# Two FFN blocks in one order: both high halves, then both low halves; a row of scales by turning a column

## The chip, the cores and the metric

One core of one Trainium2 chip. The metric is the device time of one launch in microseconds (us), the median of the runs. TensorE multiplies matrices, ScalarE applies functions and copies, VectorE does elementwise arithmetic, GpSimd and SyncE issue transfers; each works through its own program in order and waits on semaphores for the others.

## The reference

Two blocks of a model on 256 tokens of width 1024, in float32. Cut to the part that the change touches:

```python
def rms_norm(x, g):
    y = xf * lax.rsqrt(jnp.mean(xf * xf, axis=-1, keepdims=True) + RMS_EPS)
    return (y * g.astype(jnp.float32)).astype(x.dtype)

def swiglu(x, w_gate, w_up, w_down):
    return (jax.nn.silu(x @ w_gate) * (x @ w_up)) @ w_down

# first block, layers 0 and 1
h = h + 0.5 * swiglu(rms_norm(h, ffn1_norm[i]), ffn1_w_gate[i], ffn1_w_up[i], ffn1_w_down[i])
h = h + m          # layer 0: a gated recurrence, layer 1: pooling over windows
h = h + 0.5 * swiglu(rms_norm(h, ffn2_norm[i]), ...)
h = h + sigmoid(rms_norm(h, ple_norm[i]) @ ple_w_gate[i]) * (p[i] @ ple_w_proj[i])
# second block, layers 0 and 1: a mix of attention and a bidirectional recurrence, then
x = x + (jax.nn.silu(h @ w_gate[layer]) * (h @ w_up[layer])) @ w_down[layer]
```

The hidden width of every FFN is 2816. There are six FFNs: they are followed by the recurrent stage, a PLE stage (the gate with `p`), the pool, a PLE stage, a mix stage and the end of the program.

## The kernel before

Every weight matrix is read once, in blocks of 1 MB (128 partitions x 2048 float32), in the order of use. Block n is loaded into one of three raw slots, ScalarE writes its rounded high half `hi` (L455) and VectorE the rest `lo = raw - hi` (L927), each into one of three slots; TensorE multiplies both halves with the high and low parts of the activations. A block's product is x_hi w_hi + x_lo w_hi + x_hi w_lo. A slot of `hi` and `lo` comes free when TensorE has counted `block_used` for the block three before; SyncE issues a load when the block that had the raw slot has been split (`lo_ready`).

An FFN (`kind == "ffn"`, from L2102 on TensorE) has 11 chunks of 256 hidden columns. A chunk is three blocks: gate, up (both 1024 x 256) and down (256 x 1024). `feature_pairs` (L1822) does a gate or an up block: 16 matmuls of 512 columns with `w_hi` against both parts of the activations (the *highs*, L1834), then 16 of 256 columns with `w_lo` (the *lows*, L1839), then `block_used`. The gate goes into banks 0 and 1 of `psA`, the up into banks 2 and 3. `contract` does a down block into `psD`: 16 matmuls of 512 columns with `w_hi`, 8 with `w_lo` (all L1945). The down block of chunk c runs after gate and up of chunk c+1: TensorE's order is gate 0, up 0, gate 1, row of scales, up 1, down 0; then, in a loop over chunks 2 to 9, gate c, up c, down c-1; then gate 10, up 10, and `contract_last` with the last two down blocks. `contract_last` does its second block by columns when a norm or a PLE stage follows (after 24 matmuls of the first), and by rows otherwise (after 18); between its parts it turns (transposes) the new h tile by tile for the next stage.

On the other engines, in program order:

- ScalarE: `gate_half` (L593) copies the gate's second half out of `psA` when `block_used` says that the gate block is done, `up_half` (L598) the up's; `silu` (L603); `prod_high` (L608) rounds the product. In the first chunks: split, `gate_half` of chunk 1, `silu` of chunk 0, `prod_high` of chunk 0. In the last chunk: split, `gate_half`, split of the last down block, `silu`, `up_half`, split of the next stage's first block, `prod_high`.
- VectorE: `gate_sum` (L1292), `scaled_gate` (L1298, times the row of scales), `up_sum` (L1303), `gated` (L1309 the product, L1311 its low part). In the first chunks: `take_row`, `scaled_gate` of chunk 0, `gate_sum` of chunk 1, `gated` of chunk 0. In the last chunk: split, `gate_sum`, `scaled_gate`, before the pool `scale_pool` (L1093), split of the last down block, `up_sum`, `gated`, before a PLE stage one more piece (L956), split of the next block, and then the updates of h (L1373).
- The semaphores that TensorE waits for in a chunk: `gate_summed` and `up_summed` (the bank is read out), `hi_ready`, `lo_ready`, and ahead of a down block `prod_lo_ready`.

The scales of a norm (one per token, a column of `stat` per token tile, `norm_stats`, L1031) are applied after the matmul, along the columns of the result, so they are wanted as a row that stands on all partitions. VectorE makes a diagonal matrix of them, `diagonal_of` (L1095), and TensorE multiplies ones with it, `row_of_scales` (L2034, the product is L2039); VectorE copies the row out (`take_row`, L1070). This is done nine times: in each FFN, in the recurrent stage and in the two mix stages.

Of the kernel before, what the change touches and what calls it, by code (L numbers as in the profile page):

```python
# [21 lines left out]
ALU = mybir.AluOpType  # L22
# [3 lines left out]
P = 128  # L26
S = 256
T = S // P
D = 1024
KT = D // P  # L30
# [7 lines left out]
FC = 256  # L38
CH = F // FC
# [33 lines left out]
QK_T = GATE_B  # L73
SQUARES, TURNER = 22016, 22528
SCRATCH = 22784
# [16 lines left out]
def build(nc, a, out):  # L92
# [5 lines left out]
    def sem(name):  # L98
        return ctx.enter_context(nc.semaphore(name))

    with ctx:
# [38 lines left out]
        level_words = view(POOL_M, len(LEVELS), P).bitcast(I32)  # L140
        turner = view(TURNER, T, P)
        squares = view(SQUARES, 512).bitcast(mybir.dt.bfloat16).rearrange("p (c d) -> p c d", c=2)
# [12 lines left out]
        h_ready, ssq_ready, mean_ready, rms_ready = sem("h_ready"), sem("ssq_ready"), sem("mean_ready"), sem("rms_ready")  # L155
        hg_ready, turner_ready = sem("hg_ready"), sem("turner_ready")
        rstd_ready, row_done, row_ready, z_ready = sem("rstd_ready"), sem("row_done"), sem("row_ready"), sem("z_ready")
# [755 lines left out]
        def _(dve):  # L913
# [116 lines left out]

            def norm_stats(factor=None, row=True):  # L1031

                for t in range(T):
                    root(t)
                if st["renorm"]:

                    st["renorm"] = 0
                    two = lambda c: stat[:, c:c + 2]
                    step(dve.tensor_copy(two(RSTD1), two(RSTD)))
                    dve.wait_ge(ssq2_ready, 2 * T)  # L1040
                    pairs = stat[:, SSQ2:SSQ2 + 2 * T].rearrange("p (t c) -> p t c", c=2)
                    step(dve.tensor_reduce(two(SUM2), pairs, AX_X, ALU.add))
                    settle()
                    step(dve.tensor_tensor(two(SUM2), two(SUM2), two(RSTD), ALU.mult))
                    settle()
                    step(dve.tensor_tensor(two(SUM2), two(SUM2), two(RSTD), ALU.mult))
                    settle()
                    dve.memset(stat[:, 14:15], 0.0).then_inc(sum2_ready, 1)
                    dve.wait_ge(rms2_ready, 1)
                    inverse_root(D, 2, SUM2, ROOT2, V2, INV2, STEP2)  # L1050
                    step(dve.tensor_tensor(two(RSTD), two(RSTD), two(INV2), ALU.mult))
                    settle()
                if factor is not None:
                    step(dve.tensor_scalar(stat[:, FACTOR:FACTOR + 2], stat[:, RSTD:RSTD + 2], factor, None, ALU.mult))
                    settle()
                dve.memset(stat[:, 15:16], 0.0).then_inc(rstd_ready, 1)
                if row:
                    for t in range(T):
                        diagonal_of(t).then_inc(turner_ready, 1)

# [26 lines left out]
            def scale_pool():  # L1087
# [5 lines left out]
                dve.tensor_tensor(v, v, s_, ALU.mult).then_inc(pool_scaled, 1)  # L1093

            def diagonal_of(t):  # L1095
                dve.wait_ge(ident_loaded, 16)
                return dve.tensor_scalar(turner[:, t, :], ident[:], col(RSTD + t), None, ALU.mult)

# [115 lines left out]
            for stage, nxt in zip(plan, plan[1:] + [("end",)]):  # L1214
# [32 lines left out]
                if kind == "pool":  # L1247
# [16 lines left out]
                    root(0)  # L1264
                    windows_of(0).then_inc(turner_ready, 1)
                    st["update"](1, 1).then_inc(h_ready, 1)
                    biased(0, 0)
                    root(1)
                    windows_of(1).then_inc(turner_ready, 1)
                    for t, c in ((1, 0), (0, 1), (1, 1)):  # L1270
# [208 lines left out]
                if kind == "ple":  # L1479
                    norm_pieces_of(ple_pieces)  # L1480
                    for i in range(KT // 2 + 1):
                        if i < KT // 2:
                            split_to(n)
                        if i == 0:
                            norm_stats(row=False)
                        n += 1
# [279 lines left out]
        def _(pe):  # L1766
            st = {"norm": 0, "piece": 0, "ffn": 0, "updates": 0, "row": 0, "turns": None, "turn_late": False}

# [53 lines left out]
            def feature_pairs(n_at, n, bank, fresh=False, between=None):  # L1822
# [78 lines left out]
                last.then_inc(block_used, 1)  # L1901

            def tokens_first(n_at, n, bank_free):

# [129 lines left out]
            def row_of_scales():  # L2034

                st["norm"] += 1
                pe.wait_ge(turner_ready, T * st["norm"])
                for t in range(T):
                    last = pe.matmul(psD[:, 0, t * P:(t + 1) * P], one_row[:], turner[:, t, :], start=True, stop=True)  # L2039
                last.then_inc(row_done, 1)  # L2040
# [19 lines left out]
            for stage, nxt in zip(plan, plan[1:] + [("end",)]):  # L2060
                kind = stage[0]
                if kind == "norm" and n == 0:
                    turn_gains(0)
                    st["turns"] = turns_of(stage, None)
                    st["turns"](0)
                    st["turns"](1)
                    warm(6)
                    st["turns"](2)
                if kind == "pool":

                    windows = view(POOL_M, T, 4, S)
                    st["norm"] += 1
                    for t in range(T):
                        pe.wait_ge(h_ready, 2 * T * st["updates"] + 2 * (t + 1))
                        pe.wait_ge(turner_ready, T * (st["norm"] - 1) + t + 1)
                        for k in range(KT):
# [25 lines left out]
                if kind == "ffn":  # L2102
# [5 lines left out]

                    def gates(n_at, n, c_at, fresh=False):
                        pe.wait_ge(gate_summed, c_at)  # L2110
                        feature_pairs(n_at, n, 0, fresh)

                    def ups(n_at, n, c_at):
                        pe.wait_ge(up_summed, c_at)
                        feature_pairs(n_at, n, 2)

                    feature_pairs(n + 1, n, 0, fresh=True)
# [5 lines left out]

                    feature_pairs(n + 2, n + 1, 2, between=turn_params if st["ffn"] == 0 else None)
                    gates(n + 3, n + 2, c0 + 1)
                    row_of_scales()
                    if st["ffn"] == 0:
                        turn_gains(1)
                    ups(n + 4, n + 3, c0 + 1)
                    if st["ffn"] == 0:  # L2130
# [3 lines left out]
                    with pe.Fori(0, (CH - 3) // 2) as j:  # L2134
                        for e in range(2):
                            gates(6 * j + (n + 3 * e + 1), n + 3 * e, 2 * j + (c0 + e + 2))
                            ups(6 * j + (n + 3 * e + 2), n + 3 * e + 1, 2 * j + (c0 + e + 2))
                            down(6 * j + (n + 3 * e + 3), n + 3 * e + 2, 2 * j + (c0 + e + 2), 1 + e)
                    n += 3 * (CH - 3)
                    gates(n + 1, n, c0 + CH - 1)  # L2140
                    ups(n + 2, n + 1, c0 + CH - 1)
                    pe.wait_ge(prod_lo_ready, c0 + CH - 1)
# [270 lines left out]
```

## Time and profile before

| | us |
|---|---|
| median of 3 runs | 1741.14 (1740.86 to 1741.39) |
| span of the profiled execution, first to last instruction | 1739.6 |
| TensorE busy, matmuls | 1728.8 (99%) |
| TensorE weight loads, beside the matmuls | 1500.2 (86%) |
| VectorE busy | 1262.9 (73%) |
| ScalarE busy | 1003.7 (58%) |
| GpSimd busy | 58.9 (3%) |

The chain of work that ended last runs for 91% of the span on TensorE. In the profile a matmul's length includes the time that it overlaps with the next one, so the time of a group of matmuls is read from its first start to the start of what follows. In the timeline PE is TensorE, DVE VectorE, ACT ScalarE; a row is a run of like instructions with its start, its length and its count.

### The profile page before, as it was taken

To read this page: it belongs to the slowest core of one execution; us is meant where nothing else is said; L and a number is where in the kernel's file an instruction comes from. 1 tells how busy PE (TensorE), PEld (TensorE's weight loads), DVE (VectorE), ACT (ScalarE), POOL (GpSimd) and SP (SyncE) were. 2 spreads that over 40 slices of the span, in tenths; PEclk is the share of its full clock that TensorE was granted. 3 is DMA by queue.
4 is the path that set the end of the run, shared out by engine and by line. 5 is a ranking of instruction groups with operands and counts; after the bars stand their busy time and mean duration, and the time that the engine had idled before them with its cause. 6 is when DMAs were issued, how large, how long until landed. Compare 5 with 4: busy or idle time off the path is not lost.

```text
span 1739.6 us, 24239 instructions
## 1 busy us (share of the span) xinstructions
PE 1728.8 (99%) x9535; PEld 1500.2 (86%) x9535; DVE 1262.9 (73%) x1602; ACT 1003.7 (58%) x1247; POOL 58.9 (3%) x95
## 2 busy tenths in 40 slices
PE   9999999999999999999999999999999999999998
PEld 8888998888888888888889888888888988888887
DVE  6766777766677666876667898867666898876665
ACT  7544566654467444754457866464446966565444
POOL 7200000000000000000001000000000000000000
PEclk9999999999999999999999999999999999999999
DMA  7755435665545655465545544356555554446552
GB/s 244 255 189 188 162 122 170 217 222 189 191 169 181 212 187 176 144 208 185 189 145 194 184 165 145 122 186 220 190 192 170 163 176 134 138 165 215 188 186 88
DMA packets 211564, 311.65 MB, mean 179 GB/s; under 512 B 6434, under 2 KB 166112, under 8 KB 211360
## 3 DMA queue, kind: packets, MB, share of 16 engines
q1 hardware_dynamic: 207472, 303.84, 53.4%
q0 software_dynamic: 3712, 6.44, 1.2%
q8 instruction: 50, 0.82, 0.2%
q10 hardware_dynamic: 304, 0.33, 0.1%
q14 instruction: 26, 0.21, 0.0%
HBM read 309.54 MB, written 1.05 MB: 179 GB/s over the span
## 4 chain that ended last, share of the span: by engine, by line
PE 91%; ACT 4%; DVE 3%; issue 1%; DMA 0%; SPq 0%; DVEq 0%; ACTq 0%
PE psD L1945 28%; PE psA L1834 27%; PE psA L1839 14%; PE psA L1912 3%; PE psA L1927 3%; PE psA L1778 3%; PE psA L1945 2%; PE psD L2231 2%; PE psA L1931 1%; PE psA L1916 1%; PE psA L1783 1%; PE psA L2015 1%; ACT hi L455 1%; PE psD L2168 1%; PE psD L2015 1%
## 5 line engine op out<-in xcount | busy, mean ns | idle before, releaser
L927 DVE TENSOR_TENSOR lo<-raw,hi 128x2048 fp32r<-128x2048 f32 x285 | 650.5, 2290 | 171.9 <-ACT hi L455 171.2
L455 ACT ACTIVATE hi<-raw 128x2048 fp32r<-128x2048 f32 x285 | 542.4, 1909 | 77.2 <-PE psD L1945 33.5
L1834 PE MATMUL psA<-xT,hi 128*128 128x512 f32 x2094 | 501.1, 390 | 0.1
L1834 PEld LDWEIGHTS psA<-xT,hi 128*128 128x128 f32 x2094 | 387.2, 188 | 77.0 <-DVE xT L960 0.3
L1839 PEld LDWEIGHTS psA<-xT,lo 128*128 128x128 f32 x2112 | 271.9, 191 | 11.8 <-issue 0.5
L1839 PE MATMUL psA<-xT,lo 128*128 128x256 f32 x2112 | 276.8, 283 | 0.1
L1945 PE MATMUL psD<-hi,prod_hi 128*128 128x512 f32 x544 | 213.4, 392 | 0.0
L1945 PE MATMUL psD<-hi,prod_lo 128*128 128x512 f32 x544 | 212.6, 391 | 0.0
L1945 PE MATMUL psD<-lo,prod_hi 128*128 128x512 f32 x544 | 143.6, 389 | 0.0
L593 ACT ACTIVATE scr<-psA 128x512 f32<-128x512 f32 x66 | 39.3, 595 | 163.3 <-PE psA L1839 163.3
L608 ACT ACTIVATE prod_hi<-scr 128x512 fp32r<-128x512 f32 x66 | 41.7, 632 | 157.8 <-DVE scr L1309 157.8
L1945 PEld LDWEIGHTS psD<-lo,prod_hi 128*128 128x128 f32 x544 | 102.1, 188 | 21.3
L1945 PEld LDWEIGHTS psD<-hi,prod_lo 128*128 128x128 f32 x544 | 102.4, 188 | 19.4
L1945 PEld LDWEIGHTS psD<-hi,prod_hi 128*128 128x128 f32 x544 | 102.4, 188 | 19.4
L598 ACT ACTIVATE scr<-psA 128x512 f32<-128x512 f32 x66 | 39.2, 594 | 132.7 <-PE psA L1839 132.7
L1945 PE MATMUL psD<-hi,xT 128*128 128x512 f32 x368 | 101.9, 393 | 0.0
L1303 DVE TENSOR_TENSOR scr<-psA,scr 128x512 f32<-128x512 f32 x66 | 45.6, 690 | 76.1 <-ACT scr L598 76.1
L1292 DVE TENSOR_TENSOR scr<-psA,scr 128x512 f32<-128x512 f32 x66 | 45.5, 689 | 71.4 <-ACT scr L593 71.4
L1778 PE MATMUL psA<-xT,hi 128*128 128x256 f32 x704 | 89.9, 284 | 0.0
L1778 PEld LDWEIGHTS psA<-xT,hi 128*128 128x128 f32 x704 | 86.5, 191 | 0.1
L1311 DVE TENSOR_TENSOR prod_lo<-scr,prod_hi 128x512 fp32r<-128x512 f32 x66 | 45.7, 692 | 46.7 <-ACT prod_hi L608 46.7
L1945 PEld LDWEIGHTS psD<-hi,xT 128*128 128x128 f32 x368 | 67.9, 188 | 13.4
(308 smaller groups left out, 1926.2 us busy)
## 6 DMA issues: line engine op xcount, KB each, us to landing
raw<-in_w_in SPq DMA_DIRECT2D x48, 1024.0 KB, 5.2
raw<-in_ffn_w_up SPq DMA_DIRECT2D x43, 1024.0 KB, 5.4
raw<-in_ffn_w_gate SPq DMA_DIRECT2D x43, 1024.0 KB, 5.4
raw<-in_ffn_w_down SPq DMA_DIRECT2D x43, 1024.0 KB, 5.0
raw<-in_w_gate SPq DMA_DIRECT2D x22, 1024.0 KB, 5.3
raw<-in_w_up SPq DMA_DIRECT2D x22, 1024.0 KB, 5.3
raw<-in_w_down SPq DMA_DIRECT2D x22, 1024.0 KB, 4.9
raw<-in_lru_w_in SPq DMA_DIRECT2D x10, 1024.0 KB, 5.3
```

Source lines behind the costliest of these rows:

```text
L455: act.activation(hi[:, n % RING, :], raw_of(n), ACT.Copy).then_inc(hi_ready, 1)
L608: act.activation(span(prod_hi[:, c % 2]), prod[:, c % 2, :], ACT.Copy).then_inc(prod_hi_ready, 1)
L927: dve.tensor_tensor(lo[:, n % RING, :], raw_of(n), hi[:, n % RING, :].bitcast(F32), ALU.subtract).then_inc(lo_ready, 1)
L1292: dve.tensor_tensor(both(sil[:, c % 2, :]), psA[:, 0:2, 0:S], gate_l, ALU.add).then_inc(gate_summed, 1)
L1303: dve.tensor_tensor(up[:, c % 2], psA[:, 2:4, 0:S], up_l, ALU.add).then_inc(up_summed, 1)
L1311: dve.tensor_tensor(span(prod_lo[:, c % 2]), prod[:, c % 2, :], span(prod_hi[:, c % 2]).bitcast(F32), ALU.subtract).then_inc(prod_lo_ready, 1)
L1778: pe.matmul(to[:, f * S:(f + 1) * S], w_hi[:, k, f * P:(f + 1) * P], x[:, k, :], start=(begin and f == 0 and k == 0 and x is xTh), stop=False)
L1834: pe.matmul(psA[:, bank + f, :], w_hi[:, k, f * P:(f + 1) * P], xT[:, k].rearrange("p e s -> p (e s)"), start=(k == 0), stop=False)
L1839: last = pe.matmul(psA[:, bank + f, 0:S], w_lo[:, k, f * P:(f + 1) * P], xTh[:, k, :], start=(begin and k == 0), stop=(k == KT - 1))
L1912: pe.matmul(psA[:, t, :], x[:, k, t * P:(t + 1) * P], w_hi[:, k, :], start=(k == 0 and x is xTh), stop=False)
L1927: pe.matmul(psA[:, t, :], x[:, KT // 2 + k, t * P:(t + 1) * P], w_hi[:, k, :], start=False, stop=False)
L1945: last = pe.matmul(to[:, 2 * t + c, :], x[:, k, ts], w[:, k, half_of[c]], start=(first and k == 0 and e == 0), stop=(final and k == 1 and ...
```

## The change

Three parts:

- For all pairs but the first of an FFN, a new function `gates_and_ups` takes the place of a call of `gates` and one of `ups`: highs of the gate, highs of the up, lows of the gate, lows of the up. `block_used` is still counted at the end of each block's lows. The waits are the same, in the new places.
- The row of scales is made by turning (transposing) the column of `stat`, read 128 times with step zero, against the identity matrix. The diagonals, their tile `turner` and the semaphore `turner_ready` go; TensorE waits for `rstd_ready` in its place. The pool's windows, which used the same semaphore, get one of their own.
- In an FFN the row of scales (in the first FFN also the turn of the other gains) stands between the highs of chunk 1's gate and the highs of its up; it stood after the gate's lows.

The programs of ScalarE and VectorE lose the diagonals and are otherwise the same.

```diff
-            def norm_stats(factor=None, row=True):
+            def norm_stats(factor=None):
...
                 dve.memset(stat[:, 15:16], 0.0).then_inc(rstd_ready, 1)
-                if row:
-                    for t in range(T):
-                        diagonal_of(t).then_inc(turner_ready, 1)
...
-            def diagonal_of(t):
-                dve.wait_ge(ident_loaded, 16)
-                return dve.tensor_scalar(turner[:, t, :], ident[:], col(RSTD + t), None, ALU.mult)
...
+            def gates_and_ups(n_at, n, c_at, between=None):
+
+
+                def halves_of(v, m):
+                    return v[:, m % RING, :].rearrange("p (k f) -> p k f", f=FC)
+
+                def high(m, bank):
+                    w = halves_of(hi, m)
+                    for f in range(2):
+                        for k in range(KT):
+                            pe.matmul(psA[:, bank + f, :], w[:, k, f * P:(f + 1) * P], xT[:, k].rearrange("p e s -> p (e s)"),
+                                      start=(k == 0), stop=False)
+
+                def low(m, bank):
+                    w = halves_of(lo, m)
+                    for f in range(2):
+                        for k in range(KT):
+                            last = pe.matmul(psA[:, bank + f, 0:S], w[:, k, f * P:(f + 1) * P], xTh[:, k, :], start=False, stop=(k == KT - 1))
+                    last.then_inc(block_used, 1)
+
+                pe.wait_ge(gate_summed, c_at)
+                pe.wait_ge(hi_ready, n_at)
+                high(n, 0)
+                if between:
+                    between()
+                pe.wait_ge(up_summed, c_at)
+                pe.wait_ge(hi_ready, n_at + 1)
+                high(n + 1, 2)
+                pe.wait_ge(lo_ready, n_at)
+                low(n, 0)
+                pe.wait_ge(lo_ready, n_at + 1)
+                low(n + 1, 2)
...
             def row_of_scales():
 
-                st["norm"] += 1
-                pe.wait_ge(turner_ready, T * st["norm"])
+                pe.wait_ge(rstd_ready, st["rstd"])
                 for t in range(T):
-                    last = pe.matmul(psD[:, 0, t * P:(t + 1) * P], one_row[:], turner[:, t, :], start=True, stop=True)
+                    last = pe.transpose(psD[:, 0, t * P:(t + 1) * P], stat[:, RSTD + t:RSTD + t + 1].broadcast_to([P, P]), ident[:])
                 last.then_inc(row_done, 1)
...
-                    gates(n + 3, n + 2, c0 + 1)
-                    row_of_scales()
-                    if st["ffn"] == 0:
-                        turn_gains(1)
-                    ups(n + 4, n + 3, c0 + 1)
+
+                    def rows_turned():
+
+                        row_of_scales()
+                        if st["ffn"] == 0:
+                            turn_gains(1)
+
+                    gates_and_ups(n + 3, n + 2, c0 + 1, rows_turned)
...
                     with pe.Fori(0, (CH - 3) // 2) as j:
                         for e in range(2):
-                            gates(6 * j + (n + 3 * e + 1), n + 3 * e, 2 * j + (c0 + e + 2))
-                            ups(6 * j + (n + 3 * e + 2), n + 3 * e + 1, 2 * j + (c0 + e + 2))
+                            gates_and_ups(6 * j + (n + 3 * e + 1), n + 3 * e, 2 * j + (c0 + e + 2))
                             down(6 * j + (n + 3 * e + 3), n + 3 * e + 2, 2 * j + (c0 + e + 2), 1 + e)
                     n += 3 * (CH - 3)
-                    gates(n + 1, n, c0 + CH - 1)
-                    ups(n + 2, n + 1, c0 + CH - 1)
+                    gates_and_ups(n + 1, n, c0 + CH - 1)
```

## Rows read from the trace of the kernel before

**Rows 1.** The page, part 1: busy us of TensorE and the others.
```profile
PE 1728.8 (99%) x9535; PEld 1500.2 (86%) x9535; DVE 1262.9 (73%) x1602; ACT 1003.7 (58%) x1247; POOL 58.9 (3%) x95
```
**Rows 2.** Waits of TensorE: us in total, times, longest; the first of six rows.
```profile
PE psD L2054 <- DVE one_row L1131: 1.1, 1, 1.1
```
**Rows 3.** TensorE's timeline, a middle chunk: start us, length, instruction, count.
```profile
39.52 3.79 PE L1834 MATMUL psA<-xT,hi 128*128 128x512 f32 x16
43.15 2.08 PE L1839 MATMUL psA<-xT,lo 128*128 128x256 f32 x16
45.06 3.82 PE L1834 MATMUL psA<-xT,hi 128*128 128x512 f32 x16
48.72 2.08 PE L1839 MATMUL psA<-xT,lo 128*128 128x256 f32 x16
50.63 0.40 PE L1945 MATMUL psD<-hi,prod_hi 128*128 128x512 f32 x1
```
**Rows 4.** TensorE's timeline in the second FFN, chunk 1 to its first down.
```profile
316.68 0.64 PE L1839 MATMUL psA<-xT,lo 128*128 128x256 f32 x4
317.16 3.82 PE L1834 MATMUL psA<-xT,hi 128*128 128x512 f32 x16
...
322.73 0.60 PE L2039 MATMUL psD<-scr,one_row 128*128 128x128 f32 x4
323.09 3.91 PE L1834 MATMUL psA<-xT,hi 128*128 128x512 f32 x16
...
328.75 0.40 PE L1945 MATMUL psD<-hi,prod_hi 128*128 128x512 f32 x1
```
**Rows 5.** Timeline of three engines in the first FFN's last chunk.
```profile
177.65 3.82 PE L1834 MATMUL psA<-xT,hi 128*128 128x512 f32 x16
177.85 0.60 ACT L593 ACTIVATE scr<-psA 128x512 f32<-128x512 f32 x1 [3.21 <-PE psA L1839]
178.34 1.91 ACT L455 ACTIVATE hi<-raw 128x2048 fp32r<-128x2048 f32 x1
180.28 2.29 DVE L927 TENSOR_TENSOR lo<-raw,hi 128x2048 fp32r<-128x2048 f32 x1 [0.39 <-ACT hi L455]
...
188.69 0.39 PE L1945 MATMUL psD<-hi,prod_hi 128*128 128x512 f32 x1
...
190.25 0.75 DVE L1373 SCALAR_TENSOR_TENSOR h<-psD,stat,h 128x512 f32<-128x512 f32 x1 [0.98 <-PE psD L1945]
191.41 0.60 PE L2015 MATMUL psA<-ident,h 128*128 128x128 f32 x4
```
**Rows 6.** The page, part 6: DMA issues, count, KB each, us to landing.
```profile
raw<-in_ffn_w_gate SPq DMA_DIRECT2D x43, 1024.0 KB, 5.4
```
**Rows 7.** Timeline of ScalarE and VectorE ahead of the second FFN's first down.
```profile
325.25 0.58 ACT L593 ACTIVATE scr<-psA 128x512 f32<-128x512 f32 x1
...
326.47 0.68 DVE L1309 TENSOR_TENSOR scr<-scr 128x512 f32<-128x512 f32 x1
...
327.85 0.69 DVE L1311 TENSOR_TENSOR prod_lo<-scr,prod_hi 128x512 fp32r<-128x512 f32 x1 [0.70 <-ACT prod_hi L608]
```
**Rows 8.** Timeline of TensorE and ScalarE in the first FFN, chunk 1.
```profile
22.25 3.82 PE L1834 MATMUL psA<-xT,hi 128*128 128x512 f32 x16
...
25.19 3.71 ACT L455 ACTIVATE hi<-scr 128x2048 fp32r<-128x2048 f32 x2
```
**Rows 9.** VectorE's timeline in the last chunk before the pool.
```profile
689.81 2.28 DVE L1093 TENSOR_TENSOR raw<-raw,scr 128x2048 f32<-128x2048 f32 x1
```
**Rows 10.** Timeline of VectorE and TensorE in the first mix stage.
```profile
950.73 0.28 DVE L1097 TENSOR_SCALAR scr<-ident,stat 128x128 f32<-128x128 f32 x1
...
951.26 0.71 PE L2039 MATMUL psD<-scr,one_row 128*128 128x128 f32 x4
```
**Rows 11.** TensorE's timeline at the start of the program.
```profile
1.14 4.21 PE L2054 MATMUL psD<-one_row 128*128 128x128 f32 x18 [1.14 <-DVE one_row L1131]
...
7.24 1.50 PE L2054 MATMUL psD<-one_row 128*128 128x128 f32 x12
```

More of the change, by code:

```diff
@@ L73 @@
 QK_T = GATE_B
-SQUARES, TURNER = 22016, 22528
+SQUARES = 22016
 SCRATCH = 22784
@@ L140, in build @@
         level_words = view(POOL_M, len(LEVELS), P).bitcast(I32)
-        turner = view(TURNER, T, P)
         squares = view(SQUARES, 512).bitcast(mybir.dt.bfloat16).rearrange("p (c d) -> p c d", c=2)
@@ L155, in build @@
         h_ready, ssq_ready, mean_ready, rms_ready = sem("h_ready"), sem("ssq_ready"), sem("mean_ready"), sem("rms_ready")
-        hg_ready, turner_ready = sem("hg_ready"), sem("turner_ready")
+        hg_ready, windows_ready = sem("hg_ready"), sem("windows_ready")
         rstd_ready, row_done, row_ready, z_ready = sem("rstd_ready"), sem("row_done"), sem("row_ready"), sem("z_ready")
@@ L1264, in _ @@
                     root(0)
-                    windows_of(0).then_inc(turner_ready, 1)
+                    windows_of(0).then_inc(windows_ready, 1)
                     st["update"](1, 1).then_inc(h_ready, 1)
@@ L1268, in _ @@
                     root(1)
-                    windows_of(1).then_inc(turner_ready, 1)
+                    windows_of(1).then_inc(windows_ready, 1)
                     for t, c in ((1, 0), (0, 1), (1, 1)):
@@ L1484, in _ @@
                         if i == 0:
-                            norm_stats(row=False)
+                            norm_stats()
                         n += 1
@@ L1766, in _ @@
         def _(pe):
-            st = {"norm": 0, "piece": 0, "ffn": 0, "updates": 0, "row": 0, "turns": None, "turn_late": False}
+            st = {"piece": 0, "ffn": 0, "updates": 0, "rstd": 0, "turns": None, "turn_late": False}
             def features(n_at, n, to, fresh=False):
@@ L2068, in _ @@
                     st["turns"](2)
+                if kind in ("ffn", "lru", "ple", "mix"):
+                    st["rstd"] += 1
                 if kind == "pool":
                     windows = view(POOL_M, T, 4, S)
-                    st["norm"] += 1
                     for t in range(T):
                         pe.wait_ge(h_ready, 2 * T * st["updates"] + 2 * (t + 1))
-                        pe.wait_ge(turner_ready, T * (st["norm"] - 1) + t + 1)
+                        pe.wait_ge(windows_ready, t + 1)
                         for k in range(KT):
@@ L2107, in down @@
                         contract(n_at, n, prod_hi[:, c % 2], prod_lo[:, c % 2], psD, first)
[L2109 to L2115, printed above, removed]
                     feature_pairs(n + 1, n, 0, fresh=True)
```

## Prediction, made before the changed kernel was run

> **What bounds the kernel now.** I read the page's busy times first, then TensorE's own waits, then TensorE's timeline through one chunk, and last ScalarE and VectorE at the two ends of an FFN. TensorE is busy 1728.8 of a span of 1739.6 us [rows 1]; its longest wait is 1.1 us, at the start [rows 2]. So there is hardly a stall to remove: the change can gain by making TensorE's stream shorter, and lose by opening a wait. In a middle chunk [rows 3] the gate highs take 39.52 to 43.15, 3.63 us; the gate lows 1.91; the up highs 45.06 to 48.72, 3.66; the up lows 1.91; no wait shows. The reader should see that the work is one unbroken stream on TensorE, and that the question is which product, split or copy comes late once its order is changed.
>
> **The stream itself.** There are 60 pairs in the new order (10 in each of 6 FFNs; the first pair of an FFN keeps its own). The matmuls are the same. The second highs now follow highs, not lows: 3.63 for 3.66 us [rows 3], some 0.025 us a pair, 60 x 0.025 = -1.5 us. A run of 32 lows is not in the trace. Its one end is 1.91 us for 16, as now (nothing gained); its other end is half the pace of a 512-column matmul, 3.63/16/2 = 0.113 us, so 16 x 0.113 = 1.81 and 0.096 us saved in each of 120 halves, -11.5 us. I take the first end: the last four lows of a run take 0.48 us, 0.12 each (316.68 to 317.16 [rows 4]), so a run does not become faster as it goes on.
>
> In the loop nothing else opens. A gate's lows now end one group of highs (3.63 us) later, so ScalarE's copy of the gate's second half, VectorE's sum, the split of the block that takes the slot over, and on SyncE's queue the load behind that split each move by up to that. They are followed by the up lows and the down block, 1.91 + 5.47 us (183.22 to 188.69, where 183.22 is 177.65 + 3.66 + 1.91 [rows 3, 5]), before the slot or the bank is wanted. A copy of 0.60, a split of 1.91 on ScalarE and of 2.29 on VectorE [rows 5] fit there, and the product is wanted only by the down block one chunk on, some 11 us further. A load lands 5.4 us after its issue [rows 6] and its block is taken up a chunk (16 us) later. I cost the loop at nothing; without that cover a late step would cost its lateness in each of 48 rounds.
>
> **The first down block of each FFN.** Here the cover goes. The first down needs the product of chunk 0. In ScalarE's queue SiLU of chunk 0 stands behind the copy of chunk 1's gate half, and in VectorE's queue that product stands behind chunk 1's gate sum; both wait for the end of chunk 1's gate lows, and the diff leaves both queues' order alone. From the copy's start at 325.25 to the end of the product's low part at 327.85 + 0.69 = 328.54 the chain takes 3.29 us [rows 7]; the copy starts 0.20 us after the lows (177.65 to 177.85 [rows 5]), and for the hand-over to TensorE I estimate 0.08 (of the 1.38 us from 326.47 to 327.85 [rows 7], 0.68 and a ScalarE step of 0.6 leave 0.1 for two). So the down may start 3.57 us after the gate lows. Before, row, up highs and up lows lay between, 322.73 to 328.75 = 6.02 us [rows 4], and hid the chain. Now only the up lows do, 1.91 us: a wait of 1.66. Counted from the start of the gate highs: before 317.16 to 328.75 = 11.59; now 3.66 + row 0.2 + up highs 3.75 (323.09 to 328.75 less 1.91 [rows 4]) + gate lows 1.91 + 3.57 = 13.09. That is +1.5 us in each of five FFNs, 7.5.
>
> In the first FFN there is more. The up highs come 1.91 us earlier and want the high half of their block, the first of the two splits that ScalarE starts at 25.19, behind the statistics [rows 8]; it ends at 25.19 + 1.91 = 27.10. The gate highs start at 22.25, so with the row and one turn for the gains TensorE is there at 22.25 + 3.66 + 0.3 = 26.2, and waits 0.9. That FFN pays 2.4. In the others the split is done before. Together **+9.9 us**.
>
> **The last chunk of each FFN.** I count from the end of the gate lows. The copy starts at 0.20, ScalarE's split of the last down block 0.49 behind it (178.34), to 2.6; VectorE's split of that block from 2.63 to 4.92 (180.28 [rows 5]). Before, the up lows came 5.57 us after the gate lows, when this split was over. Now they come after 1.91, and VectorE's up sum waits behind the split: up sum 4.8 to 5.5, product 5.6 to 6.3, its low part 7.0 to 7.7 (offset 1.38 and lengths 0.69 as in [rows 7]). The last down block wants it at 1.91 + 5.47 = 7.4: with the hand-over 0.4 late. Behind it VectorE splits the next stage's first block, 7.6 to 9.9, and only then updates h, 9.8 to 10.5 (0.75, at 190.25 [rows 5]); TensorE's first turn comes 2.72 us after the last block's start (188.69 to 191.41) and is 0.1 late. That is 0.5 each for the two FFNs before a norm, 1.0. Before a PLE stage one more VectorE step of 0.69 stands ahead of that split, and the turn is 0.7 to 0.8 late: two times, 1.6. Where rows come first (before the pool, and at the end of the program) the product is wanted after 18, not 24, matmuls, at 1.91 + 4.1 = 6.0: 1.7 us late at the end; before the pool VectorE scales the pool's weights first, 2.28 us [rows 9], less what overlaps of starts give back, so 3.5 late. Together **+7.8 us**.
>
> **The row of scales.** Four passes in 0.36 us (322.73 to 323.09 [rows 4]) become two turns; I take 0.18 saved in each. The six in the FFNs are in the sum above. The one in the recurrent stage gives 0.2; in the two mix stages TensorE now doesn't wait for the diagonals, two steps of 0.28 from 950.73, with the row at 951.26 [rows 10], so 0.5 each: **-1.2 us**. A turn of a column read with step zero is not in the trace. Its bounds are half of the old row (as taken) and the whole of it (then -0.6 here, and +1.1 in the FFNs). VectorE's other diagonals lay beside other work.
>
> **Sum.** -1.5 + 9.9 + 7.8 - 1.2 = +15.0 us: the profiled span goes from 1739.6 to 1754.6. The median of the runs, 1741.14, lies 1.5 above that span; with the same edge, **1756.1 us**.
>
> **Rivals.**
> (1) *The lows speed up.* If the pace of a low is a price of switching between 512 and 256 columns that a run of 32 doesn't pay, the other end above applies: 1756.1 - 11.5 = 1744.6, just within 0.2% of before, so not slower. It decides against my sign from 0.21 us gained a pair, and reaches zero at 0.275. For it: such a run is untried; against it, the 0.12 us of the last four lows [rows 4].
> (2) *The ends are covered.* If the up sum did not stand behind the split in the last chunks, the 7.8 us would go: 1748.3. Against it: that order is written out in VectorE's program, and the split's input is there at 2.6 us.
> (3) *The clock falls in the new waits.* At the start 18 small matmuls take 4.21 us, 234 ns each; the same matmul takes 125 ns later, 12 in 1.50 us [rows 11]. So the first stretch ran at the lower of the two levels (1.2, not 2.4 GHz), at a cost of 18 x 0.109 = 2.0 us. A wait of 3.5 us, as before the pool, is not in the trace; if it brings the lower level back for a stretch like that, it costs 2.0 more: 1758.1. Bounds 0 and 2.0 each for that wait and the one in the first FFN; I take 0, since the page's longest wait, 1.1 us [rows 2], lies in that first stretch and tells nothing of it.
> The Trainium skill, "TensorE: Matmul & The Clock Gate", Part 1, says that the throttled level is the engine's default and that idleness brings it back, which speaks for this rival. No row of this case shows such a fall.
>
> **How the numbers follow.** Forecast 0.74; rival 1 0.10, half of it beyond the point where the kernel is faster by over 0.2%, half within; rival 2 0.06; rival 3 0.10. A measurement can tell some 0.2%, 3.5 us. So slower 0.90, same 0.05, faster 0.05. The range goes from 1749 (half of the lows' gain, or most of the ends covered) to 1761 (the clock, a dear turn, and 2 us of hand-overs mis-sized).
>
> **What would show it.** Right: waits of some 1.6 us on the product's low part ahead of six first down blocks, of 1.7 us at the last chunk and 3.5 us before the pool, of 0.9 us for the high half in the first FFN, and 32 lows in 3.8 us. Wrong: no such wait, lows near 0.113 us, or a lower granted clock behind a wait.

## The result, and the profile after

The changed kernel takes 1758.8 us (median of runs from 1757.3 to 1759.05) where the kernel before takes 1741.0; the ratio is 1.0099, 95% interval 1.0087 to 1.0112. It is slower by 1%, as forecast (1756.1, range 1749 to 1761). The profiled run is 1758.81 us long with a span of 1757.0; the span grew by 17.4 us, where the sum said 15.0. One run of a kernel further down took 2459.69 us at a mean granted clock of 0.65, and no figure here rests on it.

The page of the kernel after, part 1, in the order of [rows 1]: TensorE's busy time is the same within 0.5 us, so nearly all of the growth is waiting.

```profile
PE 1729.3 (98%) x9517; PEld 1497.9 (85%) x9517; DVE 1250.7 (71%) x1584; ACT 998.6 (57%) x1247; POOL 59.5 (3%) x95
```

TensorE's waits in the kernel after (us in total, times, longest). In [rows 2] the longest was 1.1 us. Here a down block waits ten times for a product's low part (the "issue" is one of them, in the first FFN), and once the up highs wait for the high half:

```profile
PE psD L1970 <- DVE prod_lo L1303: 13.1, 9, 3.4
PE psD L1970 <- issue: 1.5, 1, 1.5
...
PE psA L1905 <- ACT hi L454: 0.7, 1, 0.7
```

The timeline of TensorE in the second FFN, kernel after, from chunk 1's gate highs to the first down, to be held against [rows 4]:

```profile
319.76 3.82 PE L1905 MATMUL psA<-xT,hi 128*128 128x512 f32 x16
323.41 0.38 PE L2063 MATMUL psD<-ident,stat 128*128 128x128 f32 x2
323.55 3.89 PE L1905 MATMUL psA<-xT,hi 128*128 128x512 f32 x16
327.27 3.99 PE L1912 MATMUL psA<-xT,lo 128*128 128x256 f32 x32
332.75 0.50 PE L1970 MATMUL psD<-hi,prod_hi 128*128 128x512 f32 x1 [1.48 <-DVE prod_lo L1303]
333.08 0.40 PE L1970 MATMUL psD<-hi,prod_lo 128*128 128x512 f32 x1
```

It takes 332.75 - 319.76 = 12.99 us to the first down, 1.40 more than before, and the down's second matmul comes 0.33 us behind its first (332.75 to 333.08). Before, that step was 0.23, from 328.75 [rows 4] to this row:

```profile
328.98 0.40 PE L1945 MATMUL psD<-hi,prod_lo 128*128 128x512 f32 x1
```

So the place costs 1.50 us in this FFN, and as much in three others; in the third it costs 1.34, because there the step was 0.33 before the change too. ScalarE and VectorE in the same stretch, kernel after, show why, as [rows 7] did for before. The gate lows end about 327.27 + 1.91 = 329.18; the copy of the gate half starts at 329.38, and everything that chunk 0's product needs is lined up behind it, to the low part's end at 332.00 + 0.69:

```profile
329.38 0.60 ACT L592 ACTIVATE scr<-psA 128x512 f32<-128x512 f32 x1 [1.52 <-PE psA L1912]
329.88 0.62 ACT L602 ACTIVATE scr<-scr 128x512 f32<-128x512 f32 x1
330.02 0.69 DVE L1284 TENSOR_TENSOR scr<-psA,scr 128x512 f32<-128x512 f32 x1 [4.07 <-ACT scr L592]
330.62 0.68 DVE L1301 TENSOR_TENSOR scr<-scr 128x512 f32<-128x512 f32 x1
331.34 0.63 ACT L607 ACTIVATE prod_hi<-scr 128x512 fp32r<-128x512 f32 x1 [0.84 <-DVE scr L1301]
...
332.00 0.69 DVE L1303 TENSOR_TENSOR prod_lo<-scr,prod_hi 128x512 fp32r<-128x512 f32 x1 [0.69 <-ACT prod_hi L607]
```

The same stretch of the first FFN, TensorE, kernel after. The up highs start 0.99 us after the turn of the gains, because the split that [rows 8] shows is not done; the whole takes 36.44 - 22.34 = 14.10 us where before it took 33.97 - 22.25 = 11.72 (its start is in [rows 8], its end is the first row here):

```profile
33.97 0.47 PE L1945 MATMUL psD<-hi,prod_hi 128*128 128x512 f32 x1
```
```profile
22.34 3.82 PE L1905 MATMUL psA<-xT,hi 128*128 128x512 f32 x16
26.00 0.38 PE L2063 MATMUL psD<-ident,stat 128*128 128x128 f32 x2
26.21 0.25 PE L2073 MATMUL psD<-ident,scr 96*128 96x96 f32 x1
27.20 3.88 PE L1905 MATMUL psA<-xT,hi 128*128 128x512 f32 x16 [0.74 <-ACT hi L454]
30.91 3.99 PE L1912 MATMUL psA<-xT,lo 128*128 128x256 f32 x32
36.44 0.47 PE L1970 MATMUL psD<-hi,prod_hi 128*128 128x512 f32 x1 [1.53 <-issue]
```

The last chunk of the first FFN, three engines, kernel after (before: [rows 5]). VectorE's split of the last down block, from 186.18, lies ahead of its up sum at 188.39, though TensorE finished the up lows at 185.47 already. The product's low part, from 190.57, comes after the last block is due, and TensorE stands still for 0.31 us before 191.41:

```profile
183.75 0.60 ACT L592 ACTIVATE scr<-psA 128x512 f32<-128x512 f32 x1 [5.94 <-PE psA L1912]
184.25 1.91 ACT L454 ACTIVATE hi<-raw 128x2048 fp32r<-128x2048 f32 x1
...
185.47 0.40 PE L1970 MATMUL psD<-hi,prod_hi 128*128 128x512 f32 x1
...
186.18 2.29 DVE L926 TENSOR_TENSOR lo<-raw,hi 128x2048 fp32r<-128x2048 f32 x1 [0.38 <-ACT hi L454]
...
188.39 0.68 DVE L1295 TENSOR_TENSOR scr<-psA,scr 128x512 f32<-128x512 f32 x1
...
190.57 0.69 DVE L1303 TENSOR_TENSOR prod_lo<-scr,prod_hi 128x512 fp32r<-128x512 f32 x1 [0.70 <-ACT prod_hi L607]
...
191.41 0.47 PE L1970 MATMUL psD<-hi,prod_hi 128*128 128x512 f32 x1 [0.31 <-DVE prod_lo L1303]
```

Ahead of the pool the same wait is the longest, since VectorE also scales the pool's weights first ([rows 9]). The busy times by stretch there, kernel after: start and end us; length; busy us and count of PE, PEld, DVE, ACT, POOL; the granted clock of TensorE; share of the DMA engines and GB/s. The first stretch holds the wait, and the second shows what the sum had left at nothing: the granted clock is 0.50, the lower of the two levels.

```profile
702.85:708.00 5.15, 1.75 (x8) 1.19 (x7) 4.35 (x5) 2.81 (x4) 0.00 (x0) 0.99 0.62 189
708.00:711.30 3.30, 3.30 (x10) 2.52 (x9) 0.95 (x2) 0.00 (x0) 0.00 (x0) 0.50 0.41 109
711.30:720.00 8.70, 8.58 (x44) 7.14 (x43) 7.68 (x20) 6.03 (x14) 0.00 (x0) 1.00 0.25 88
```

TensorE's timeline there, kernel after: behind a wait of 3.40 us the matmuls first start 0.227 us apart, and from 708.24 to 711.22 seven times 0.427 us (2.98); with the two steps at the edges, 0.39 and 0.28, that costs 7 x 0.20 + 0.16 + 0.05 = 1.6 us.

```profile
706.63 0.47 PE L1970 MATMUL psD<-hi,prod_hi 128*128 128x512 f32 x1 [3.40 <-DVE prod_lo L1303]
706.95 0.39 PE L1970 MATMUL psD<-hi,prod_lo 128*128 128x512 f32 x1
707.17 0.39 PE L1970 MATMUL psD<-lo,prod_hi 128*128 128x512 f32 x1
...
708.24 0.63 PE L1970 MATMUL psD<-hi,prod_hi 128*128 128x512 f32 x1
...
711.22 0.44 PE L1970 MATMUL psD<-hi,prod_lo 128*128 128x512 f32 x1
711.50 0.40 PE L1970 MATMUL psD<-lo,prod_hi 128*128 128x512 f32 x1
```

A middle chunk on TensorE in the kernel after (before: [rows 3]): highs of both blocks in 49.21 - 41.96 = 7.25 us, both lows in 53.05 - 49.21 = 3.84, that is 0.120 us each.

```profile
41.96 7.42 PE L1905 MATMUL psA<-xT,hi 128*128 128x512 f32 x32
...
49.21 4.00 PE L1912 MATMUL psA<-xT,lo 128*128 128x256 f32 x32
53.05 0.40 PE L1970 MATMUL psD<-hi,prod_hi 128*128 128x512 f32 x1
```

Holding the starts of the same matmuls in both traces against each other, place by place, divides the 17.4 us:

| place | forecast | measured |
|---|---|---|
| first down blocks, with the row of scales between | +9.9 (2.4 + 5 x 1.5) | +9.8 (2.38 + 1.34 + 4 x 1.51) |
| ends: two norms, two PLE stages | +2.6 (2 x 0.5 + 2 x 0.8) | +2.6 (0.59 + 0.60 + 0.69 + 0.71) |
| end before the pool | +3.5 | +5.0 |
| end of the program | +1.7 | +1.9 |
| other pairs, in the loop and behind it | -1.5 | -1.1 |
| rows of scales outside the FFNs | -1.2 | -0.9 |
| ahead of the first gate highs of chunk 1 | 0 | +0.1 |
| sum | +15.0 | +17.4 |

### The profile page after: what moved, and what is told of

Its sections match the earlier page's. It is cut to its first block, busy times and chain, and to the rows that moved or that the text cites. A ratio compares the mean times of both kernels' runs of the same rounds, so it can differ in the third digit from the quotient of the medians.

```text
span 1757.0 us, 24185 instructions
## 1 busy us (share of the span) xinstructions
PE 1729.3 (98%) x9517; PEld 1497.9 (85%) x9517; DVE 1250.7 (71%) x1584; ACT 998.6 (57%) x1247; POOL 59.5 (3%) x95
## 4 chain that ended last, share of the span: by engine, by line
PE 86%; ACT 6%; DVE 5%; issue 2%; DMA 1%; SPq 0%; DVEq 0%; ACTq 0%
PE psD L1970 26%; PE psA L1905 25%; PE psA L1912 12%; PE psA L1937 3%; PE psA L1952 3%; PE psA L1770 3%; ACT hi L454 2%; PE psA L1826 2%; PE psA L1970 2%; PE psD L2249 2%; PE psA L1956 1%; PE psA L1941 1%; DVE lo L926 1%; PE psA L1775 1%; PE psA L2040 1%
## 5 line engine op out<-in xcount | busy, mean ns | idle before, releaser
L1905 PE MATMUL psA<-xT,hi 128*128 128x512 f32 x1920 | 446.5, 389 | 0.7 <-ACT hi L454 0.7
L1905 PEld LDWEIGHTS psA<-xT,hi 128*128 128x128 f32 x1920 | 359.5, 188 | 75.0 <-DVE scr L1295 0.9
L1912 PEld LDWEIGHTS psA<-xT,lo 128*128 128x128 f32 x1920 | 238.3, 192 | 4.7
L1912 PE MATMUL psA<-xT,lo 128*128 128x256 f32 x1920 | 239.7, 283 | 0.0
L592 ACT ACTIVATE scr<-psA 128x512 f32<-128x512 f32 x66 | 39.5, 598 | 329.8 <-PE psA L1912 325.9
L1284 DVE TENSOR_TENSOR scr<-psA,scr 128x512 f32<-128x512 f32 x66 | 45.6, 691 | 229.7 <-ACT scr L592 229.7
L1770 PEld LDWEIGHTS psA<-xT,hi 128*128 128x128 f32 x704 | 86.5, 192 | 0.1
L1952 PE MATMUL psA<-hi,xT 128*128 128x512 f32 x288 | 72.5, 394 | 0.0
L1937 PE MATMUL psA<-hi,xT 128*128 128x512 f32 x288 | 70.7, 397 | 0.0
```

The lines of the kernel that those rows point to most:

```text
L592: act.activation(gate_l, psA[:, 0:2, S:2 * S], ACT.Copy).then_inc(gate_l_ready, 1)
L1284: dve.tensor_tensor(both(sil[:, c % 2, :]), psA[:, 0:2, 0:S], gate_l, ALU.add).then_inc(gate_summed, 1)
L1770: pe.matmul(to[:, f * S:(f + 1) * S], w_hi[:, k, f * P:(f + 1) * P], x[:, k, :], start=(begin and f == 0 and k == 0 and x is xTh), stop=False)
L1905: pe.matmul(psA[:, bank + f, :], w[:, k, f * P:(f + 1) * P], xT[:, k].rearrange("p e s -> p (e s)"), start=(k == 0), stop=False)
L1912: last = pe.matmul(psA[:, bank + f, 0:S], w[:, k, f * P:(f + 1) * P], xTh[:, k, :], start=False, stop=(k == KT - 1))
L1937: pe.matmul(psA[:, t, :], x[:, k, t * P:(t + 1) * P], w_hi[:, k, :], start=(k == 0 and x is xTh), stop=False)
```

## Experiments

The theory: the stream on TensorE is nearly as long as before, and the loss comes from two places where ScalarE and VectorE do their steps in an order that was right for the old order of TensorE, plus the clock behind the longest wait. Rivals: the new order costs something in itself (the loop, the long runs), or the turn of a column does.

**Undo one chunk at a time.** Three kernels have the old order in chunk 1, in the last chunk, or in both; the loop's eight pairs per FFN stay new. A fourth has the old order everywhere and keeps only the turned column. The function and its uses:

```diff
+            def gates_then_ups(n_at, n, c_at, between=None):
+                pe.wait_ge(gate_summed, c_at)
+                feature_pairs(n_at, n, 0)
+                if between:
+                    between()
+                pe.wait_ge(up_summed, c_at)
+                feature_pairs(n_at + 1, n + 1, 2)
...
# chunk 1 old
-                    gates_and_ups(n + 3, n + 2, c0 + 1, rows_turned)
+                    gates_then_ups(n + 3, n + 2, c0 + 1, rows_turned)
...
# last chunk old
-                    gates_and_ups(n + 1, n, c0 + CH - 1)
+                    gates_then_ups(n + 1, n, c0 + CH - 1)
```

Chunk 1 old: 

> The changed kernel with one part undone: chunk 1 of each FFN goes back to gate highs, gate lows, row of scales, up highs, up lows. Theory Q (the first down block waits because the queues of ScalarE and VectorE tie chunk 0's product to the end of chunk 1's gate lows): the waits of about 1.65 us before six first down blocks go, and the 0.9 us for the first FFN's up block; from the starts of the gate highs to the first downs the change cost 2.4 us in the first FFN and 1.4 in five others, and the turned row gives 0.2 in each, so 1758.8 - 9.4 - 1.3 = 1748.1 us. Rival P (the price is one of the pairs themselves, wherever they stand): 6 of 60 pairs undone give 17.8 / 10 = 1.8 back, 1757.0 us.

Measured 1748.65 us (1747.71 to 1749.45), ratio 1.0042 (1.0027 to 1.0058), 10.2 under the changed kernel; the queue theory said 1748.1, the rival 1757.0. The waits of the six first downs are gone but for 0.19 us in the third FFN. The other four waits of TensorE for a product in this kernel are those of the ends, the pool's 3.4 us the longest:

```profile
PE psD L1978 <- DVE prod_lo L1303: 5.9, 5, 3.4
```

Last chunk old: 

> The changed kernel with the last chunk of each FFN in the old order. Theory Q: the waits at the six ends go (0.5 before a norm, 0.7 before a PLE stage, 3.6 before the pool, 1.9 at the end of the program), together 7.9 us, and with the wait before the pool the lower granted clock behind it, 1.6 us more: 1758.8 - 9.5 = 1749.3 us, with one granted clock level from start to end. If the clock fell for another reason than that wait: 1750.9. Rival P: 1757.0 us.

Measured 1749.03 us (1748.64 to 1749.86), ratio 1.0048 (1.0033 to 1.0063), 9.8 under the changed kernel. The numbers on record were 1749.3 (the clock counted), 1750.9 (without it) and 1757.0 (the order costs in itself); the one with the clock is nearest. Its waits for a product are the six first downs alone, none over 1.5 us.

Both old: 

> The changed kernel with chunk 1 and the last chunk of each FFN in the old order; only the 48 loop chunks have both highs first, and the rows of scales are turned columns. Theory Q: no new wait of TensorE is left; the loop gives 0.02 us a chunk and costs 0.08 once in each of five FFNs (-0.7 in all), the rows give 0.2 in each of six FFNs and 0.9 in the other stages (-2.2): 1741.0 - 2.9 = 1738.1 us, faster than before. Rival P: 12 of 60 pairs undone, 1758.8 - 3.6 = 1755.2 us.

Measured 1738.61 us (1737.79 to 1739.18) beside 1741.08 for the kernel before: ratio 0.9987 (0.9978 to 0.9996). The theory said 1738.1, the rival 1755.2. So this kernel, which keeps the new order in the loop and the turned column, is 0.13% faster than the kernel before and 1.1% faster than the changed one, and its trace has no wait above 0.2 us that the kernel before did not have.

Only the turned column: 

> The old order of all pairs, and of the change only the turned column for the row of scales, at its old place behind the gate's lows. Each row is 0.2 us shorter on TensorE, nine times, and in the two mix stages TensorE no longer waits for the diagonals: 1741.0 - 2.2 = 1738.8 us. If turning a column with step zero were as dear as the old product: the mix stages' waits alone, 1740.4 us. The difference to the run with the new order in the loop alone is the loop's own worth: theory 0.7 us.

Measured 1739.56 us (1738.74 to 1740.02), ratio 0.9991 (0.9982 to 1.0000), between the two numbers on record, 1738.8 and 1740.4. Against the kernel before the row of scales is worth 1.5 us, at the edge of what the interval can tell from nothing. The step from here to the kernel above is the loop's new order alone: 1739.56 - 1738.61 = 0.95 us, and the spans of the two profiled runs, 1737.0 and 1736.0, say the same. In the trace with both chunks old every round of the loop gains 0.02 us, and 48 x 0.02 = 1.0.

**Leave TensorE's order, change the queues.** If the queue order is the cause in chunk 1, exchanging two steps there must remove the waits with the new order in place.

```diff
# ScalarE, chunk 1
-                    gate_half(n + 1)
                     silu(c0, 0)
                     prod_high(c0, 0)
+                    gate_half(n + 1)
# VectorE, chunk 1
                     scaled_gate(c0, 0)
-                    gate_sum(c0 + 1, 1)
                     gated(c0, 0)
+                    gate_sum(c0 + 1, 1)
```

> The changed kernel, all pairs in the new order; only the queues of ScalarE and VectorE differ in chunk 1: SiLU and the rounding of chunk 0's product stand ahead of the copy of chunk 1's gate half, and the product ahead of chunk 1's gate sum. Theory Q: the six waits of 1.65 us before the first down blocks go although TensorE's order is the changed one, the 0.9 us for the first FFN's up block stays: 1758.8 - 9.9 = 1748.9 us. Rival P (the order of the pairs itself costs the time there): 1758.8 us.

Measured 1748.24 us (1747.51 to 1748.5), ratio 1.0038 (1.0024 to 1.0052), 10.6 under the changed kernel (theory 1748.9, rival 1758.8). The timeline of the second FFN in this kernel: the product's low part is done by 327.71 + 0.69 = 328.40, ahead of the first down at 329.00, and the copy (L592) now stands behind the rounding of that product.

```profile
327.05 0.63 ACT L607 ACTIVATE prod_hi<-scr 128x512 fp32r<-128x512 f32 x1 [0.76 <-DVE scr L1301]
327.58 0.58 ACT L592 ACTIVATE scr<-psA 128x512 f32<-128x512 f32 x1
327.71 0.69 DVE L1303 TENSOR_TENSOR prod_lo<-scr,prod_hi 128x512 fp32r<-128x512 f32 x1 [0.70 <-ACT prod_hi L607]
...
329.00 0.40 PE L1970 MATMUL psD<-hi,prod_hi 128*128 128x512 f32 x1
```

The same exchange with the last chunk in the old order: 

> The changed kernel with the last chunk of each FFN in the old order and the two queue steps of chunk 1 exchanged (ScalarE: silu and prod_high of chunk 0 ahead of gate_half of chunk 1; VectorE: gated of chunk 0 ahead of gate_sum of chunk 1). Theory (the waits of first downs come from the order on the queues alone, those of the ends from the late half of the up; the two don't touch): the last chunk takes 9.8 us off 1758.8, the queues 10.6, together 1738.4 us. Rival (one removes part of the other's gain, or a wait appears in place of the one removed): 1741 us or more.

Measured 1738.58 us (1738.12 to 1739.58) beside 1741.17, ratio 0.9985 (0.9976 to 0.9994), where the sum of the two separate gains said 1738.4. So the two places are independent, and the new order in chunk 1 costs next to nothing once its queues suit it (the first FFN still waits 0.7 us for the split). This kernel and the one with both chunks old are the best here and can't be told apart.

**The wait before the pool.** One kernel moves the scaling of the pool's weights ahead of the last chunk's gate sum, where VectorE has time:

```diff
                         if b == 0:
+                            if nxt[0] == "pool":
+                                scale_pool()
                             gate_sum(c0 + CH - 1, CH - 1)
                             scaled_gate(c0 + CH - 1, CH - 1)
-                            if nxt[0] == "pool":
-                                scale_pool()
```

> The changed kernel with one step of VectorE moved: the scaling of the pool's weights (2.28 us) stands ahead of the last chunk's gate sum, where VectorE idles, not behind it. Theory Q with the clock: the wait before the pool falls from 3.6 to 1.7 us, as at the end of the program, and the granted clock then stays at its upper level: 1758.8 - 1.8 - 1.6 = 1755.4 us. If the clock falls all the same: 1757.0. If that scaling is not in the chain: 1758.8.

Measured 1755.95 us (1754.55 to 1756.27), ratio 1.0082 (1.0065 to 1.0098), 2.9 under the changed kernel; 1755.4 was for the wait and the clock, 1757.0 for the wait alone. The rows of TensorE's timeline and of the stretches behind it show a wait half as long, and a clock that stays at 1.00:

```profile
705.11 0.47 PE L1970 MATMUL psD<-hi,prod_hi 128*128 128x512 f32 x1 [1.67 <-DVE prod_lo L1303]
```
```profile
703.00:705.10 2.10, 0.44 (x2) 0.04 (x2) 1.41 (x3) 1.47 (x2) 0.00 (x0) 1.00 0.76 218
705.10:711.00 5.90, 5.89 (x26) 4.90 (x27) 4.45 (x6) 2.66 (x9) 0.00 (x0) 1.00 0.70 233
```

One more kernel, run twice, leaves the wait as long as it is and gives TensorE something to do in it; the bank that is written is idle there and nothing reads it.

```diff
+                if fill is not None:
+                    pe.wait_ge(gate_summed, fill)
+                    for _ in range(14):
+                        pe.matmul(psA[:, 0, 0:P], one_row[:], one_row[:], start=True, stop=True)
```

> The changed kernel with 14 small matmuls of ones into an idle bank put into TensorE's wait before the pool; their result is not used. They take some 3 us of the 3.6 us and move nothing else. Theory C (the lower granted clock behind that wait comes from TensorE's idleness): the clock stays at its upper level and the eight matmuls behind the wait take 0.23 and not 0.43 us each, 1758.8 - 1.6 = 1757.2 us. Rival (the clock falls for another reason, or the slow matmuls are not the clock's): 1758.8 us.

Measured 1757.65 us (four runs, 1756.85 to 1757.9), ratio 1.0094 (1.0077 to 1.0111): between 1757.2 (the clock) and the rival's 1758.8, nearer the first, too close to settle it. The trace of this run is not used. So the kernel was run again beside the changed kernel on the same chip.

> The changed kernel with 14 small matmuls of ones into an idle bank, put into TensorE's wait before the pool; the wait's end and everything else stay. Theory (the idle of 3.6 us is what the clock falls behind): no stretch of the granted clock at 0.50 behind the pool, its eight matmuls at 227 ns, 1757.2 us. Rival (the clock falls for another reason, or the fill delays what comes behind): a stretch at 0.50 remains, 1758.8 us or more.

> The changed kernel once more, to see whether its time moves with the clock behind the pool. Theory (the fall of the granted clock is one way that the wait of 3.6 us before the pool can end, and costs 1.6 us when it comes): a run without a stretch at 0.50 behind the pool takes 1757.2 us, a run with one 1758.8 us, and the trace of this run shows the one that its time says. Rival (the difference between runs has to do with other things): the trace and the time of the run don't go together.

Measured: filled 1757.24 us (1756.83 to 1757.48), ratio to the kernel before 1.0092 (1.0077 to 1.0107); the changed kernel 1759.54 (1759.04 to 1759.96), ratio 1.0106 (1.0090 to 1.0121). The runs of the two don't overlap; the difference is 2.3 us. The timeline and the stretches of the filled kernel: the fill ends at 702.39 + 3.29 = 705.68, the down block starts 705.94 - 702.39 = 3.55 us after the fill's first matmul. In the first profile of the changed kernel it starts as long after the point where a next matmul could have started (706.63 - 702.85 less one pace of 0.23, 3.55). Here the clock stays at 1.00:

```profile
702.39 3.29 PE L2020 MATMUL psA<-one_row 128*128 128x128 f32 x28
705.94 0.47 PE L1970 MATMUL psD<-hi,prod_hi 128*128 128x512 f32 x1 [0.26 <-DVE prod_lo L1303]
```
```profile
702.30:705.90 3.60, 3.38 (x30) 3.14 (x28) 2.80 (x5) 1.98 (x3) 0.00 (x0) 1.00 0.46 129
705.90:711.00 5.10, 5.06 (x22) 4.23 (x23) 4.12 (x4) 1.88 (x6) 0.00 (x0) 1.00 0.67 218
```

The same stretches of the changed kernel, run beside it, with the wait of 3.39 us up to 705.73. This time the lower clock was there at once and lasted longer, to about 711.0:

```profile
702.00:705.80 3.80, 0.41 (x3) 0.10 (x1) 3.00 (x5) 2.19 (x3) 0.00 (x0) 0.81 0.46 136
705.80:711.00 5.20, 5.20 (x13) 4.04 (x14) 1.98 (x1) 0.56 (x2) 0.00 (x0) 0.50 0.67 221
```

From 706.29 to 710.98 there are 11 steps of 0.427 us rather than 0.227, 2.2 us, and 0.3 more at the edges. Behind the pool the changed kernel is 2.4 us later against the filled one than ahead of it; the spans, 1757.2 and 1755.0, differ by 2.2, since their starts differ by 0.2. So the idle wait is what the clock falls behind, and its price differs from run to run: held against the filled kernel over the same stretch, the first profile of the changed kernel lost 1.4 us (1.6 by its steps, of which 0.2 came back) and this one 2.4. The expectation for the second run of the changed kernel had 1758.8 for a run with the fall and came out 0.7 short, because it took the price to be fixed.

The price may also be nothing. Each run, with a trace or without, has a mean granted clock. It is 0.997 or 0.998 in 16 of the 17 runs that have this wait long and unfilled (the changed kernel's two sets, chunk 1 old, the queues exchanged), and 0.999 in all 45 runs of the kernels of this section where the wait is gone or shortened, or was filled in the second of its two sets. The 17th run has 0.999 too: it is the 1757.3 us that is the lowest in the result, the time of the filled kernel. It left no trace, but time and clock read as a run in which the clock did not fall. So the long wait brings the fall in most runs and, as far as this shows, not in every one.

## Why the prediction was right, and where its terms were off

**Direction and size.** The forecast was 1756.1 and the time is 1758.8, inside the range, for the reasons given: waits at the first downs and the chunk ends, 9.8 + 2.6 + 5.0 + 1.9 = 19.3 us, against 2.0 us gained elsewhere. Of the 5.0, though, 1.4 is the lower clock, which the forecast had at nothing.

**The first downs: right.** The start of the down was forecast 3.57 us after the gate lows; it came 332.75 - 329.18 = 3.57 after them. The wait of 1.66 was measured as 1.65 (the 32 gate and up lows end at 327.27 + 32 x 0.12 = 331.1; the row's own 1.48 counts from the modelled end of the last of them), and the queue exchange showed that the order of the steps in the two queues is its cause. Two small misses cancel: the two turns take 0.14 us where I took 0.2 (323.41 to 323.55) and the up highs were 0.03 shorter, so the down's first matmul came 1.40 later and not 1.5; its second one lost the other 0.10, which I had not counted. That the six places come out so near the forecast, 9.8 for 9.9, is in so far luck. The first FFN paid 2.4, as forecast, with the wait for the split at 0.99 from start to start, forecast 0.9.

**The ends: right but for the clock.** Norms 0.59 and 0.60 for 0.5, PLE stages 0.69 and 0.71 for 0.8, the program's end 1.9 for 1.7; that the up sum waits behind the split is seen at 186.18 and 188.39. So rival 2 (the ends are covered) is refuted. Undoing the last chunk removed all of these waits; the order on VectorE's queue was exchanged by itself for the pool's scaling alone, and at the other ends its part is read from the rows. The last block before the pool was forecast 3.5 late and is 3.55.

**The clock: the term that failed.** Rival 3 said that the clock could fall in that wait, at 2.0 us, and the forecast took 0 for it, because the longest wait in the trace of before was 1.1 us and "tells nothing of it". It fell, in every trace that has this wait unfilled: the changed kernel twice, and the kernels with chunk 1 old and with the queues exchanged. It cost 1.4 us in the first profile, 2.4 in the second, and nothing in the run of 1757.3 us, as far as its mean clock tells. With 1.4 in the sum the forecast would have been 1757.5. The other wait for which I bounded this, in the first FFN, is 1.53 us long and brought no fall; the stretch behind it, kernel after, with the columns of the stretches above:

```profile
36.40:45.00 8.60, 8.56 (x38) 7.14 (x39) 6.61 (x6) 5.27 (x6) 8.60 (x18) 1.00 0.49 160
```

The Trainium skill, "TensorE: Matmul & The Clock Gate", Part 1, which the prediction quoted against its own choice, holds that the lower clock is the default and that idleness brings it back; here the traces agree as to idleness, with 0.50 behind an idle stretch of 3.4 us and 1.00 behind the same stretch filled. What failed is the step that let an absence of evidence stand for zero, though the evidence was there. [Rows 11] spoke for it by the pace, 234 against 125 ns (the profile's column of the granted clock reads 1.00 in that stretch). And "No row of this case shows such a fall" is true of the rows chosen, not of the trace of the kernel before. TensorE's last matmul there ends at 1732.64, and behind the idleness that follows the granted clock is 0.50 (columns as above):

```profile
1732.60:1737.50 4.90, 0.04 (x1) 0.00 (x0) 3.73 (x12) 1.74 (x4) 0.00 (x0) 1.00 0.29 116
1737.60:1739.60 2.00, 0.00 (x0) 0.00 (x0) 0.00 (x0) 0.00 (x0) 0.00 (x0) 0.50 0.58 222
```

**The stream: too much by 0.4.** I took 0.025 us for each of 60 pairs, -1.5. A round of the loop gains 0.02 (both highs 7.25 for 7.29, both lows 3.84 for 3.82), and the last pairs' gain is counted in the ends: -1.1 in the changed kernel, -0.95 between the two kernels that differ in the loop alone. The expectation for the kernel with both chunks old took 0.08 once in each of five FFNs off the loop's gain; in the traces of the change this is the slower first step of the first down, and no part of the loop. Rival 1 (lows speed up in a run) is refuted: 0.120 us each, the same as in a run of 16.

**The rows outside the FFNs: too much by 0.3.** The recurrent stage gave 0.24 for 0.2 and the second mix stage 0.48 for 0.5, but the first mix stage only some 0.15 for 0.5: the work behind its row came 0.52 earlier, as forecast, and most of that was lost again before the next FFN. What takes it back there was not tried. A column read with step zero costs no more than an ordinary turn: two take 0.14 us, and four turns of h tiles 0.36 (310.02 to 310.38 in the kernel after).

Together: 1.5 too little before the pool, 0.2 at the program's end, 0.4 and 0.3 too much saved in the stream and the rows, and 0.1 ahead of the first FFN's chunk 1, less 0.1 too much for the first downs, make 2.4 us, the difference of 17.4 and 15.0. The times differ by 0.3 more, 2.7, because the forecast put 1.5 us between span and time where the profiled run has 1758.8 - 1757.0 = 1.8.

## What to carry to other kernels

When TensorE's order changes, walk each other engine's queue past the new order: a step that was placed behind an early event blocks everything after it once that event comes late, and exchanging the two is worth as much as undoing the change (10.6 and 10.2 us here). A wait that the change opens is priced with the clock behind it, not only with its length: work put into it keeps the clock up, 2.3 us here, though the wait stays as long. And split a change into its places before judging it: the loop of this one gains 0.95 us, and its two ends lose 19 in each launch.

## What the runs showed of the hardware

- TensorE's granted clock was 0.50 behind an idle stretch of 3.4 us in each of four traces, for 7 to 12 matmuls of 512 columns at 0.427 us rather than 0.227, from the first matmul on or up to 1.2 us behind it; it stayed at 1.00 behind waits of 1.5 to 1.7 us. By the mean clocks the longer wait brought the fall in 16 of 17 runs. What decides between fall and no fall, no run here shows.
- 14 small matmuls of ones, in the trace 28 passes of 0.12 us, kept the clock at 1.00 through the same wait.
- The pace of a 256-column matmul against a rounded half is 0.120 us in a run of 16 and in one of 32.
